# A gated attention block in fp32: the turned quarters of mem written by GpSimd's queue, and the keys' split moved from unit 29 to unit 31

## What is computed

```python
h = _rmsnorm(x, norm_g[l])
proj = h @ w_in[l]
qa, ka, va, za, qb, kb, vb, zb, fb, qm, zm, gl = _split_cols(proj, IN_WIDTHS)
...
oa = _dilated_mixture(qa, ka, va, rel_bias)         # 12 heads, three dilations
ua = (oa * jax.nn.silu(za)) @ w_proj_a[l]
...
ob = _forgetting_attention(qb, kb, vb, log_f)       # 8 heads
ub = (ob * jax.nn.silu(zb)) @ w_proj_b[l]
mh = _rmsnorm(mem, mem_norm_g[l])
km, vm = _split_cols(mh @ w_mem_kv[l], (M_WIDTH, M_WIDTH))
...
om = _memory_attention(qm, km, vm)                  # 4 heads into mem
um = (om * jax.nn.silu(zm)) @ w_proj_m[l]
g = jax.nn.sigmoid(gl.reshape(B, S, N_BRANCH, D_MODEL) + b_gate[l])
merged = g[:, :, 0] * ua + g[:, :, 1] * ub + g[:, :, 2] * um
x = x + (merged @ w_out[l]).astype(x.dtype)
```

## Time and profile before

| | us |
|---|---|
| median of 3 runs | 1171.43 |
| lowest, highest | 1171.04, 1172.53 |
| the profiled execution, its time | 1171.77 |
| the profiled execution, its span | 1170.0 |

### The profile page before, as it was taken

The page is one execution under the profiler, slowest core; times in us unless marked ns, Lnnn a source line. Parts: engine busy times, 40 slices in busy tenths (PEclk is TensorE's granted clock), DMA queues, the critical chain, the costliest instruction groups (busy, mean ns, idle before and its releaser), DMA issues.

```text
span 1170.0 us, 14507 instructions
## 1 busy us (share of the span) xinstructions
PE 1161.8 (99%) x5307; PEld 965.8 (83%) x5307; DVE 731.5 (63%) x906; ACT 546.1 (47%) x670; POOL 44.9 (4%) x37
## 2 busy tenths in 40 slices
PE   8999999999999999999999999999999999999998
PEld 7788888888888888888888888888888888888887
DVE  6776578576566577567567555655556456555653
ACT  6565445445444545545535544435434443543432
POOL 1110000000010000000000000000000000000000
PEclk9999999999999999999999999999999999999999
DMA  9998789658568678687677786477549546755860
GB/s 335 310 282 294 258 272 336 209 186 301 179 220 294 197 251 277 203 268 232 226 259 224 247 279 215 159 225 263 186 155 300 182 163 221 253 208 202 280 243 36
DMA packets 147613, 275.85 MB, mean 236 GB/s; under 512 B 9389, under 2 KB 32613, under 8 KB 147568
## 3 DMA queue, kind: packets, MB, share of 16 engines
q1 hardware_dynamic: 135488, 258.31, 66.0%
q10 hardware_dynamic: 11600, 16.87, 4.6%
q0 software_dynamic: 480, 0.07, 0.0%
HBM read 251.34 MB, written 26.24 MB: 237 GB/s over the span
## 4 chain that ended last, share of the span: by engine, by line
PE 96%; DMA 2%; SPq 1%; DVE 1%; issue 0%; ACT 0%; DVEq 0%
PE acc L1341 31%; PE acc L1342 31%; PE acc L1343 31%; DMA w_raw<-in_w_in_dram 1%; DMA turned_mem<-group 1%; PE side L1385 1%; PE side L1377 0%; PE side L1401 0%; PE side L1410 0%; PE side L1412 0%; PE side L1408 0%; PE side L1386 0%; SPq L308 0%; SPq L312 0%; DVE group L1079 0%
## 5 line engine op out<-in xcount | busy, mean ns | idle before, releaser
L871 DVE TENSOR_TENSOR w_lo<-w_raw,w_hi 128x1024 fp32r<-128x1024 f32 x407 | 495.8, 1222 | 372.1 <-ACT w_hi L551 371.4
L551 ACT ACTIVATE w_hi<-w_raw 128x1024 fp32r<-128x1024 f32 x407 | 429.6, 1060 | 540.8 <-PE acc L1343 524.0
L1341 PE MATMUL acc<-w_hi,hT_hi 128*128 128x512 f32 x1152 | 450.0, 391 | 0.4 <-DVE w_lo L871 0.4
L1343 PE MATMUL acc<-w_hi,hT_lo 128*128 128x512 f32 x1152 | 448.4, 389 | 0.0
L1342 PE MATMUL acc<-w_lo,hT_hi 128*128 128x512 f32 x1152 | 448.3, 389 | 0.0
L1341 PEld LDWEIGHTS acc<-w_hi,hT_hi 128*128 128x128 f32 x1152 | 216.3, 188 | 46.8 <-DVE w_lo L871 1.9
L1343 PEld LDWEIGHTS acc<-w_hi,hT_lo 128*128 128x128 f32 x1152 | 216.2, 188 | 45.3
L1342 PEld LDWEIGHTS acc<-w_lo,hT_hi 128*128 128x128 f32 x1152 | 216.3, 188 | 44.0
L1341 PE MATMUL acc<-w_hi,mT_hi 128*128 128x512 f32 x256 | 99.8, 390 | 0.0
L1342 PE MATMUL acc<-w_lo,mT_hi 128*128 128x512 f32 x256 | 99.6, 389 | 0.0
L1343 PE MATMUL acc<-w_hi,mT_lo 128*128 128x512 f32 x256 | 99.6, 389 | 0.0
(11 more groups left out here) (179 smaller groups left out, 573.0 us busy)
## 6 DMA issues: line engine op xcount, KB each, us to landing
w_raw<-in_w_in_dram SPq DMA_DIRECT2D x142, 1024.0 KB, 6.4
w_raw<-in_w_mem_kv_dram SPq DMA_DIRECT2D x16, 1024.0 KB, 5.5
w_raw<-in_w_out_dram SPq DMA_DIRECT2D x16, 1024.0 KB, 5.2
w_raw<-in_w_proj_a_dram SPq DMA_DIRECT2D x12, 1024.0 KB, 5.0
w_raw<-in_w_proj_m_dram SPq DMA_DIRECT2D x8, 1024.0 KB, 5.1
w_raw<-in_w_proj_b_dram SPq DMA_DIRECT2D x8, 1024.0 KB, 5.1
turned_oz<-group SPq DMA_DIRECT2D x44, 128.0 KB, 4.7
group<-turned_oz SPq DMA_DIRECT2D x11, 512.0 KB, 5.0
```

The costliest lines, as they stand in the source:

```text
L551: act.activation(whi[:, s % RING], raw[:, slot, UK * (s % 2):UK * (s % 2) + UK], ACT.Copy)\
L871: dve.tensor_tensor(wlo[:, s % RING], raw[:, (s // 2) % RING, UK * (s % 2):UK * (s % 2) + UK], whi[:, s % RING].bitcast(F32), ALU.subtract ...
L1341: pe.matmul(banks[t][:], hi, whi[:, s % RING, j], start=first and j == 0, stop=False)
L1343: return pe.matmul(banks[t][:], lo, whi[:, s % RING, j], start=False, stop=last and j == UK - 1)
```

## The change

The four writes of mem's turned quarters leave SyncE's program. GpSimd issues them: the first quarter ahead of the root of norm 0, the other three between the root of norm 0 and the root of norm 1. The waits (`mem_turned`) and the signal (`mem_out`) are the same. `U_KSPLIT` is 31 for all groups, where it was 29.

```diff
@@ -91,7 +91,7 @@
-U_QSPLIT, U_KSPLIT, U_VSPLIT, U_PSPLIT = 24, 29, 30, 15
+U_QSPLIT, U_KSPLIT, U_VSPLIT, U_PSPLIT = 24, 31, 30, 15
...
-            def mem_write(c):
-
-                sp.wait_ge(pre["mem_turned"], c + 1)
-                spread(mem_dram[c], mem_squares, pre["mem_out"])
-
...
-                        if i in (7, 8, 10):
-                            mem_write((7, 8, 10).index(i))
...
                         if i == 12:
-                            mem_write(3)
                             mem_read(1)
...
+            def mem_write(c):
+
+                pool.wait_ge(pre["mem_turned"], c + 1)
+                for i in range(4):
+                    rows = slice(32 * i, 32 * i + 32)
+                    pool.dma_start(mem_dram[c][:, i].rearrange("(j p) n -> p j n", j=4),
+                                   mem_squares[rows].rearrange("p (j n) -> p j n", j=4)).then_inc(pre["mem_out"], 16)
+
             for i in range(2 * M_GROUPS + 2):
+                for c in ((0,), (1, 2, 3))[i] if i < 2 else ():
+                    mem_write(c)
                 pool.wait_ge(means, i + 1)
```

## The result

The changed kernel takes 1179.82 us (median of 5 runs, 1178.53 to 1182.87) where the kernel before takes 1172.18 beside it (1171.04 to 1173.76). The ratio of the two is 1.0069, 95% interval [1.0058, 1.0081]. It is slower by some 8 us, and outside the range of 1170.4 to 1175.8 that was given. The profiled execution took 1179.82 us, and its span is 7.7 us longer than that of before.

The account below looks back on a forecast made before the run. TensorE, busy 1161.8 of 1170.0 us, was taken as the bound. Keys 0, SyncE freed 0, unit 12 -0.6 and units 15 and 18 +1.4 gave +0.8 on 1171.43: 1172.3 us, range 1170.4 to 1175.8.

Parts of the forecast that it names:

- Part 1, keys: Keys split at unit 31: ScalarE's 3.83 us wait in group 0 goes, TensorE gains and loses 0.
- Part 2, SyncE freed: Four times four issues of 1.82 to 1.96 us leave SyncE; earlier weights are worth 0 to TensorE.
- Part 3, landing: GpSimd's writes of mem's quarters land 0.8 us later than SyncE's, half of the 1.6 seen on loads.
- τ: Time of one quarter's write on GpSimd, first issue to landing of all four DMAs: 8.5 us, from 7.4 to 10.8.
- Part 3, issuing: Four issues on GpSimd take 2.3 us per quarter against 1.96 on SyncE, 0.3 more.
- The added wait behind the root: GpSimd's second write stands behind the first norm's root and so starts 3.9 us later; the change's real price.
- The formula, 3τ - 24.7: Time against before at unit 18, never below -0.6; +0.8 us at 8.5 us per write, break-even at 8.2.
- Unit 12: TensorE's late start there, waiting for w_lo, goes: 0.6 us gained, the most the change can give back.
- Rival 3: GpSimd's writes land as slowly as its loads: +3.2 us, up to +7.7 (1179.1), at unit 18; chance 0.24.
- Rival 4: VectorE's w_lo delays each issue of three GpSimd writes, 2.4 us per write: +8 us, 1179.4; chance 0.03.
- τ over 10.8: Sign of a wrong prediction: a GpSimd quarter-write taking longer than 10.8 us from first issue to landing.
- A wait after 70 us: Sign of a wrong prediction: TensorE waiting in any place later than 70 us.

Follow-up runs that it names:

- e1: The kernel before with only the keys' split moved from unit 29 to 31; 1171.97 us, ratio 1.0004.
- e3: The changed kernel with 2048 instead of 1024 bytes of room for GpSimd's DMAs, and the small tile vec_rows moved into oh; 1175.59 us, ratio 1.0031.
- e8: The changed kernel with room 2048, the first three quarters written by GpSimd and the fourth by SyncE as before; 1172.83 us, ratio 1.0007.
- e5: The changed kernel with 1536 instead of 1024 bytes of room for GpSimd's DMAs; 1178.17 us, ratio 1.0052.
- e7: The changed kernel with room 2048 and GpSimd's second write ahead of the first norm's root instead of behind it; 1172.08 us, ratio 1.0001.
- e4: The changed kernel with 28 unused transposes ahead of TensorE's wait for unit 15, to keep it busy; 1177.51 us, ratio 1.0055.
- e2: The changed kernel with the keys' split back at unit 29, so only the writes moved; 1179.80 us, ratio 1.0071.
- e6: The changed kernel with only mem's first quarter written by GpSimd, the other three by SyncE as before; 1171.63 us, ratio 0.9999.
- e9: The changed kernel with each quarter written as eight DMAs of 16 rows in place of four of 32; 1181.14 us, ratio 1.0083.
- e10: The changed kernel with bf loaded three times, to three places, ahead of the root of x; 1178.79 us (one run).

## Why the prediction was wrong, point by point

- **Part 1, keys: 0.** Right (e1). ScalarE's 3.83 us are gone: in the profile after it rounds the keys at 107.72 without a wait, and TensorE doesn't wait at the scores of 116.84.
- **Part 2, SyncE freed: 0.** In the changed kernel's profile TensorE waits for no weight. But SyncE isn't as free as the part has it: its third read of mem still waits for the fourth write, now GpSimd's, and goes at 85.71 where it went at 74.23, 3.7 us more than the delay of 7.8 around it. No term stood for that, and e3 against e8 puts 2.8 us on the fourth write in another order. The part was not tried alone.
- **Part 3, landing: right.** Taken was τ = 8.5; without a pause it measured 7.3 to 9.1 (the changed kernel and e8). GpSimd's queue brings a write of 128 KB pieces home as quickly as SyncE's (7.4 to 9.7).
- **Part 3, issuing: this step failed.** It took four issues at 0.58 us from the load of `bf`, 2.3 us in all. A single issue does cost 0.55. But it was a price per instruction, from ten loads that went out without a pause, from 19.36 to 24.62 us. What it left out is that the issues draw on a room which holds seven of these sixteen DMAs (e3 and e5 moved the pause with it). In its place stood 2.2 us of issues and 6.9 us of standing still in the second write. The upper bound of 10.8 for τ fell with it: 13.5.
- **The added wait behind the root, 3.9 us: right.** e7, without it, has no wait at units 15 and 18; e8, with it, has 0.6 and 1.3.
- **The formula, 3τ - 24.7.** It holds for three equal τ without a pause. With 13.5 in the second write `w_lo` of unit 15 comes at 60.06 + 3.1 = 63.2, and TensorE is 4.3 us late there by the same working. Unit 18 doesn't wait then, since TensorE itself is late.
- **No term for the clock.** The sum carried idle time at its own length. At 4.3 us it cost another 2.5, with a granted clock of 0.52 in the 6 us behind it, while behind waits of 0.9 (e8, e4), 1.4 (e3) and 1.75 us (e2) the granted clock was 1.00.
- **Unit 12: -0.6.** Gone in the trace, but worth less than that, since e1's execution doesn't have it either.
- **Rival 3** (slow landings) is refuted by the τ without a pause, though its upper end, 1179.1, is near the measured time. **Rival 4** (VectorE holds GpSimd up) came close too, with 1179.4. Both numbers are luck. Against rival 4: VectorE stood idle from 49.1 to 60.1 us, through nearly the whole pause (48.3 to 55.2), and the pause moved with the room. Its 2.4 us were to come at each write; the first and the third had none.
- **The signs to watch.** "τ over 10.8" came true and pointed to the place at once. "A wait after 70 us" did not, in the changed kernel. The second root started at 77.51, where 69.23 and the delay of 7.8 are 77.0: 0.5 us late from the second pause, and TensorE waited for nothing behind it. By the sign's own words (69.5 plus the delay, 77.3) it came true by 0.2 us.

**Still open**: what makes the late waits of 1.4 to 1.75 us near 106 to 109 us in e2 and e3, which the profiles of the changed kernel, e7 and e8 don't have; the 1.4 to 2.2 us of the loss that the changed kernel's profile doesn't explain; and the 1.5 us in the program's first microseconds. No version beat the kernel before: e6, which has its only stall removed, measures the same.

## What to carry to other kernels

Before you move DMAs to GpSimd's queue, count them against the room that the program sets. Here 1024 bytes held 7 DMAs of 32 rows or 12 of 16 rows, 1536 held 10 and 2048 held 14 of 32 rows, and behind that count GpSimd stood for 3.6 to 7.1 us, about until those in flight had landed; for DMAs of another shape the number has to be tried. What matters is which DMA the pause falls on and who waits for that one: the pause cost some 6 us in the second write, and in the last it cost nothing in e7, while e3 with it is 2.8 us slower than e8 without. And look at the granted clock behind a long wait of TensorE: the one of 4.3 us cost 2.5 us more than its length.

## What the runs showed of the hardware

- With the room at 1024, 1536 and 2048 bytes GpSimd stood after 7 (the changed kernel), 10 (e5) and 14 (e3, e7) DMAs of 32 rows, and with 1024 after 12 of 16 rows (e9). The pauses were 3.6 (the changed kernel) to 7.1 us (e4) long. The profile shows them only as idle time with "issue" as its releaser.
- Two more loads ahead of the first write didn't count toward it (after seven in e10, too), and DMAs that had landed did (in the changed kernel the first write's four, landed by 41.33, in the seven that end at 48.3).
- An idle stretch of 4.3 us was followed by 13 matmul steps of 0.43 us on average in place of 0.24 (the changed kernel and e4), with the granted clock at 0.52 over 6 us. One of 2.6 and one of 0.9 us together (e5) were followed by about eight steps of 0.43, with the granted clock at 0.74 from 69 to 75 us. Behind single waits of 0.9 (e4, e8), 1.4 (e3) and 1.75 us (e2) it was 1.00.
- A DMA on GpSimd's queue took 0.55 us to issue with 128 KB (the changed kernel) and 0.51 with 64 KB (e9), so halving them nearly doubled the issue time of a quarter (2.25 to 4.12 us).
